# Where VectorE takes the modulation units of the first block's heads, and where TensorE sums them

## The reference

```python
c_act = jax.nn.silu(c)
for l in range(DEPTH):                       # 2 layers
    ada = c_act @ w_ada[l] + b_ada[l]        # [1024] @ [1024, 3072]
    shift, scale, gate = jnp.split(ada, 3, axis=-1)
    h = rmsnorm(x, norm_g[l]) * (1.0 + scale[:, None, :]) + shift[:, None, :]
    p = h @ w_in[l]                          # 9 parts of 1024 columns, and two of 4
    mq, mk, mv, mo, mz, mi, mf, rq, rk, rv, rz = split_cols(p)
    ...                                      # conv and silu of mq, mk; mLSTM cell of 4 heads; y_m
    ret = retention_chunkwise(rotary(rq), rotary(rk), rv)   # 4 heads; y_r
    x = x + gate[:, None, :] * (concatenate([y_m, y_r]) @ w_out[l])
```

## Time and profile before

| | us |
|---|---|
| median of three runs | 2177.64 |
| lowest, highest | 2177.52, 2178.55 |
| the profiled execution | 2177.91 |
| span of that execution in the trace | 2176.1 |
| mean granted TensorE clock in it | 0.988 of full speed |

### The profile page before, as it was taken

One profiled execution on the slowest core, in us unless ns is written; L12 is line 12 of the kernel. 1 busy time (PEld: TensorE's weight loads), 2 busy tenths in 40 slices (PEclk: granted clock), 3 DMA queues, 4 the chain that ended last, 5 costly groups with the idle time before them and its releaser, 6 DMA issues.

```text
span 2176.1 us, 33858 instructions
## 1 busy us (share of the span) xinstructions
PE 2119.0 (97%) x13613; PEld 1866.2 (86%) x13613; DVE 1749.7 (80%) x2143; ACT 1334.7 (61%) x1278; POOL 31.0 (1%) x60
## 2 busy tenths in 40 slices
PE   7999999999999999999999999999999999999998
PEld 5899999899999889999977888888888888888887
DVE  4978865877766878887878888888888888888887
ACT  3565554556645753434756776766777767776775
POOL 3000000000000000000000000000000000000000
PEclk8999999999999999999999999999999999999999
DMA  9777855566646548987456999999999999999995
GB/s 320 234 227 227 242 188 168 181 210 198 205 166 211 175 143 287 306 308 259 149 178 229 354 350 342 367 348 341 350 341 373 338 340 346 359 357 337 354 337 192
DMA packets 356160, 595.06 MB, mean 273 GB/s; under 512 B 10376, under 2 KB 201368, under 8 KB 356008
## 3 DMA queue, kind: packets, MB, share of 16 engines
q1 hardware_dynamic: 352864, 586.92, 78.7%
q0 software_dynamic: 2752, 5.86, 1.2%
q10 hardware_dynamic: 392, 0.13, 0.0%
HBM read 591.80 MB, written 4.22 MB: 274 GB/s over the span
## 4 chain that ended last, share of the span: by engine, by line
PE 83%; DVE 9%; ACT 3%; issue 3%; DMA 2%; SPq 0%; DVEq 0%; ACTq 0%
PE ps L1590 9%; PE ps L1592 9%; PE ps L1591 9%; PE ps L1119 6%; PE ps L1120 6%; PE ps L1121 6%; PE ps L1619 5%; PE ps L1620 5%; PE ps L1621 5%; PE ps L1144 2%; PE ps L1145 2%; PE ps L1146 2%; DVE wlo L1687 2%; DVE acc L1735 2%; ACT whi L701 1%
## 5 line engine op out<-in xcount | busy, mean ns | idle before, releaser
L1687 DVE TENSOR_TENSOR wlo<-raw,whi 128x2048 fp32r<-128x2048 f32 x485 | 1109.7, 2290 | 280.2 <-ACT whi L701 263.2
L701 ACT CAST whi<-raw 128x2048 fp32r<-128x2048 f32 x485 | 927.3, 1912 | 405.7 <-PE ps L1592 141.4
L1119 PE MATMUL ps<-hhi,whi 128*128 128x256 f32 x1424 | 411.3, 289 | 2.1 <-DVE wlo L1687 1.8
L1120 PE MATMUL ps<-hlo,whi 128*128 128x256 f32 x1424 | 403.4, 283 | 0.0
L1121 PE MATMUL ps<-hhi,wlo 128*128 128x256 f32 x1424 | 403.2, 283 | 0.0
L1590 PE MATMUL ps<-whi,xghi 128*128 128x512 f32 x896 | 364.1, 406 | 0.5 <-DVE wlo L1687 0.5
L1592 PE MATMUL ps<-wlo,xghi 128*128 128x512 f32 x896 | 353.9, 395 | 0.0
L1591 PE MATMUL ps<-whi,xglo 128*128 128x512 f32 x896 | 353.8, 395 | 0.0
L1119 PEld LDWEIGHTS ps<-hhi,whi 128*128 128x128 f32 x1424 | 273.5, 192 | 10.0 <-issue 7.0
L1120 PEld LDWEIGHTS ps<-hlo,whi 128*128 128x128 f32 x1424 | 273.6, 192 | 0.3
L1121 PEld LDWEIGHTS ps<-hhi,wlo 128*128 128x128 f32 x1424 | 273.4, 192 | 0.0
(11 more groups left out here) (381 smaller groups left out, 2987.9 us busy)
## 6 DMA issues: line engine op xcount, KB each, us to landing
raw<-in_moe_w_gate_dram SPq DMA_DIRECT2D x112, 1024.0 KB, 5.6
raw<-in_moe_w_up_dram SPq DMA_DIRECT2D x112, 1024.0 KB, 5.7
raw<-in_moe_w_down_dram SPq DMA_DIRECT2D x112, 1024.0 KB, 5.0
raw<-in_w_in_dram SPq DMA_DIRECT2D x92, 1024.0 KB, 5.3
raw<-in_w_ada_dram SPq DMA_DIRECT2D x69, 1024.0 KB, 7.8
raw<-in_w_out_dram SPq DMA_DIRECT2D x24, 1024.0 KB, 5.1
raw<-in_ffn_w_gate_dram SPq DMA_DIRECT2D x11, 1024.0 KB, 8.8
raw<-in_ffn_w_up_dram SPq DMA_DIRECT2D x11, 1024.0 KB, 8.3
```

Of the source, the lines that this page charges most:

```text
L701: nc.scalar.copy(whi[:, u.hl, :], raw[:, u.raw, :]).then_inc(hi_ready, 1)
L1119: mm(ps2[u.bank][:, j], whi[:, u.hl, w], hhi[:, k], start=k == 0, stop=False)
L1120: mm(ps2[u.bank][:, j], whi[:, u.hl, w], hlo[:, k], start=False, stop=False)
L1687: V.tensor_tensor(wlo[:, u.hl, :], raw[:, u.raw, :], whi[:, u.hl, :].bitcast(F32), ALU.subtract).then_inc(raw_free, 1)
```

## The change

Two tables take the place of the rules. `ADA_BESIDE` says at which step DVE takes each modulation unit, and `ADA_SUMMED` behind which step PE sums it. In layer 0 DVE now takes units 0 to 8 at steps 1, 4, 5, 7, 8, 10, 13, 14, 16, and PE sums them at 4, 6, 7, 8, 10, 11, 15, 16, 17 (before 3, 4, 6, 8, 10, 12, 14, 16, 17). In layer 1 DVE's steps are the same as before; PE's were 3, 6, 9, 12, 15, 17 and are 4, 6, 8, 12, 15, 17. DVE's places at steps 2, 3 and 6 of a head are gone, and that of step 5 lies behind the first rotation instead of ahead of it. SP's load of a modulation unit waits for DVE's `ada_free` of the unit three before it where that one was summed by DVE in the heads or beside the feed-forward, and for PE's `ada_done` elsewhere.

```diff
+ADA_BESIDE = ((1, 4, 5, 7, 8, 10, 13, 14, 16), (1, 4, 7, 10, 13, 16))
+ADA_SUMMED = ((4, 6, 7, 8, 10, 11, 15, 16, 17), (4, 6, 8, 12, 15, 17))
...
 def ada_beside(l, j):
 
-    if l == 0:
-        return {1: 0, 15: 8}.get(j, j // 2 if 0 < j < 16 and j % 2 == 0 else None)
-    return j // 3 if j >= 0 and j % 3 == 1 else None
+    return ADA_BESIDE[l].index(j) if j in ADA_BESIDE[l] else None
...
+def ada_summed(l, j):
+
+    return ADA_SUMMED[l].index(j) if j in ADA_SUMMED[l] else None
...
             def ada_load(a, block, l, at):
                 if a.n >= ADA_START:
-                    sp.wait_ge(ada_done, a.count(1 - HALF))
+                    last = Ada(a.n - HALF, 0)
+
+                    if ADA_START <= last.n < A_MIX0 or A_FF <= last.n < A_MIX1:
+                        sp.wait_ge(ada_free, last.sums())
+                    else:
+                        sp.wait_ge(ada_done, last.count())
...
                     def ada_after(j):
 
-                        at = h_no % 2 * HEAD_UNITS + j
-                        i = ada_beside(l, at - (1 if l and at == 2 * HEAD_UNITS - 1 else 2))
+                        i = ada_summed(l, h_no % 2 * HEAD_UNITS + j)
...
                     low(v.plus(LOOK))
                     if h_no == 0:
                         ada_after(1)
-                    ada_after(2)
                     if h_no:
                         retention_finish(hd.before)
                     low(o.plus(LOOK))
-                    ada_after(3)
...
-                    ada_after(5)
                     if hd.n == 0:
                         dve.wait_ge(sin_ready, 2)
                     rotate(hd, rq, 0)
+                    ada_after(5)
                     dve.wait_ge(var_done, hd.count(2, 1))
                     V.tensor_tensor(den[:], den[:], ps2[3][:, 0], ALU.add).then_inc(spread_ready, 1)
                     low(rk.plus(LOOK))
-                    ada_after(6)
                     rotate(hd, rk, 1)
```

## The result

| | us |
|---|---|
| before, median of 4 runs | 2178.1 (2177.52 to 2179.36) |
| changed, median of 4 runs | 2164.75 (2163.96 to 2167.59) |
| ratio, with its 95% interval | 0.9942 (0.9929 to 0.9954) |
| forecast | 2167.7, range 2164.2 to 2173.2 |

A forecast was written before the change was run, and what follows sets the result against it. PE, busy 2119.0 of 2176.1 us, was taken to bound the kernel. Terms of 5.8 + 0.5 + 3.6 = 9.9 us off 2177.91 gave 2168.0, stated as 2167.7 since the runs' median lies 0.27 lower; range 2164.2 to 2173.2.

The forecast's parts named there:

- a kernel without slow phases: All heads touched, clock never falling behind the gaps: 5.8 + 3.4 + 4.5 = 13.7 us won, 2163.9 us.
- heads 1 to 3 of layer 0: DVE's unit goes behind `sT`, so PE's waits for `sT` and the rotated keys go: 5.8 us, bounds 4.0 and 5.8.
- head 0 of layer 0: Values start 3.37 us earlier behind a 5.3 us gap; slow phase costs 2.9: net 0.5 us, bounds -1.0 and +2.0.
- head 0 of layer 1: Values start 4.5 us earlier behind a 2.3 us gap, 0.9 off for the clock: 3.6 us, bounds 1.7 and 4.5.
- feed-forward: Beside the feed-forward PE hardly waits, so the change wins nothing there.
- The slots: Rival: DVE can't start units because their slots aren't summed yet; some 2 us of gain left, 2175.6 us; chance 0.04.
- new wait: Rival, heads 1 to 3: wait at second rotation or `sT` leaves 1.0 to 2.0 of 5.8 us; 2172 us; chance 0.10.
- the next head's `low(k)`: Slower rival: units at steps 5 and 7 delay second rotation and next `low(k)`, 20.2 us lost, 2188 us; chance 0.03.
- The rival of the slow phases: Slow phases cost 4.4 us in layer 0's head 0, 2.8 in layer 1's: 6.5 us won, 2171.1; chance 0.13.

The follow-up runs named there:

- the kernel with the sum back: The changed kernel with PE's sum of unit 0 behind step 3 again in both layers: 2169.41 us, ratio 0.9955 to before.
- Step 6 against step 7: The changed kernel with layer 0's modulation units of step 7 (units 3 and 8) on DVE at step 6 again: 2167.20 us, ratio 0.9942 to before.
- the angles: First head's rotary angles moved behind the weighted scores, on the changed kernel with no modulation unit ahead of those scores in both layers: 2158.91 us, ratio 0.9907.
- The loads alone: The kernel before with only SP's loads of modulation units changed, to wait for DVE's sums: 2178.57 us, ratio 0.9998.
- second profile: The changed kernel itself, unaltered, profiled in another run: 2164.92 us, ratio 0.9939 to before.

## Why the prediction was right, and what it missed

The mechanisms in the heads were as told, and one place was missed. The size was too small: 13.4 us against 9.9, near the lower end of the stated range of times. That end stood for a run with hardly a slow phase. The measured time lies there for another reason: a slow phase did follow the gap in layer 0 each time, and heads 1 to 3 and the feed-forward gave 2.6 us more than the sum had for them. That the gain is close to the 13.7 us worked out for a kernel without slow phases is chance. Step by step, with the first profile of the changed kernel and, where it differs, the second:

| term | forecast | measured |
|---|---|---|
| heads 1 to 3 of layer 0 | 5.8 | 7.2 |
| head 0 of layer 0 | 0.5 | 1.3; 0.5 |
| head 0 of layer 1 | 3.6 | 4.5; 2.9 |
| feed-forward | 0 | 1.2 |
| sum | 9.9 | 14.2; 11.8 |

- **Heads 1 to 3.** All waits for `sT` and for rk went, as forecast, and DVE's order alone did it (the kernel with the sum back). The term was too small by 1.4 us. For 0.9 of it the reason is that it added the idle times as the view of waits gives them, and each of the five stalls cost more than its idle time: twice 2.11 us for 1.85, 1.18 for 1.02, twice 0.66 for 0.56, by the starts of the units around them. Step 6 against step 7 gives the same from the other side, 0.75 us lost for a wait of 0.6. The rest is the sums' new places, which I had costed at nothing: in heads 1 and 3 two sums that had taken 0.45 us each take 0.34 and 0.36.
- **Head 0 of layer 0.** The gap of 5.3 us stood where it was worked out, and the slow phase behind it came each time. The one uncertain size was the clock's, 2.9 us with bounds of 4.4 and 1.4. With the angles moved, z to rq takes 9.22 us at full clock with a gap of 1.25. With the gap of 5.25 in its place and 0.36 for the sum it would be 13.6; it is 15.30 and 15.45, and rq to rk adds 0 and 0.7. So the phase cost 1.7 us in the first profile and 2.6 in the second. What it left is not all gain: a sum that had stood ahead of rq now stands behind rv and takes 0.45 us there, one more effect of the sums' places, which had been put at nothing.
- **Head 0 of layer 1.** 4.5 us with a full clock and 2.9 with a slow phase, against bounds of 4.5 and 1.7. The even chance I gave the phase stands: in seven profiles with this gap it came in three. An even chance of 1.4 to 2.8 us is worth 1.05 us, not the 0.9 that the sum took off.
- **Feed-forward.** "PE hardly waits, so nothing there either" was the step that failed. It went by PE's waits, and the view gave 0.2 us for the sums there. By the starts around them three sums came some 0.4 us late, with ACT held up for 54.4 us by transfers behind SP's queue. The loads alone win the 1.23 us.
- **The rivals.** The slots never held DVE up (no wait of it for a sum in the heads), no new wait took the old ones' place, and PE never waits for the next head's `low(k)`. The rival of the slow phases had both phases, as the second profile has, but at 4.4 and 2.8 us, where that profile shows 2.6 and 1.6.

The profiled execution itself shows 13.95 us, not 14.2 and 0.7 more: its start-up was 1.2 us longer than in the profile of before, by chance. The medians differ by 13.4.

Behind the gap in layer 0's head 0 of the first profile, PEclk is 0.82 over 9.72 us (the row from 84.03 to 93.75, above). The Trainium skill ("TensorE: Matmul & The Clock Gate", Part 1) has the penalty of a slow phase as its length times one minus the granted share, by which 0.18 x 9.72 = 1.75 us is an estimate for this one. The stretches leave 1.7, so the trace agrees. In the second profile the estimate is 0.28 x 9.65 = 2.7 us, and the stretches leave 2.6.

## What to carry to other kernels

When an engine waits for another's late work, the wait need not vanish if the waiting step is moved behind the next product: it can move to the next thing that hangs on the same late work. Moving the sum alone turned 3.8 us of waiting into 8.3 in one layer and won 4.5 us in the other, and which of the two it would be could be read from what DVE still had to do before `sT`. So take the work out from ahead of what is waited for, and move the wait as well, and look for what fills the hole: a place that looks like 3.4 us of work may be 1.9 us of a wait for another engine.

## What the runs showed of the hardware

- A stall of PE costs more than its idle time by 0.10 to 0.26 us at full clock: 0.26 at the values, 0.16 behind the sum in head 2, 0.10 at the retention's scores. In the timelines successive matmuls overlap, and across a stall they don't; that this is the reason is not shown.
- Behind a gap of 1.25 us (three times) the clock stayed full, behind 2.29 us it fell in three of seven profiles, behind 4.2 us and more in all eight. Where it fell behind 2.29 us it cost 1.6 us each time; behind 5.25 us, 1.5 to 2.9 (five profiles).
- Ahead of the units that follow a norm PE idles for 2.7 us at three places. Where the clock then stays full (10 of 36 cases in the twelve profiles), PE soon stands another 1.2 us for `wlo`; where it falls, it doesn't. The slow phase there takes the place of a wait of about its own cost, and the time is the same. At a fourth place the idle time is 3.15 us, the clock fell each time, and in two profiles (the loads alone, the angles) the mixer took 0.9 us longer with a longer phase.
